# Gated linear attention in a one-core network kernel: chunk states replaced by scores of all tokens, small products moved between the weight products

## The chip, the core and the metric

The kernel runs on one core of a Trainium2 chip. TensorE (PE) multiplies, VectorE (DVE) and ScalarE (ACT) work element by element, SyncE (SP) issues the transfers; each works through its own queue in order and waits on semaphores of the others. The metric is the device time of one execution in microseconds (us), as the median of several.

## What is computed

A network of two transformer-like parts on 256 tokens of width 1024: two layers of feed-forward, attention or DeltaNet, and cross attention, then four layers, of which the third (i = 2) is the gated linear attention (GLA) that is changed. `first_block`, retention, convolution and MLP layers stand around it untouched.

```python
def gated_linear_scan(q, k, v, log_g, strict):      # heads 4, dk 128, dv 256, chunks of 64 of the 256 tokens
    c = jnp.cumsum(lg, axis=3)                       # inside a chunk
    c_last = c[:, :, :, -1:, :]
    q_dec, k_dec, k_end = q * jnp.exp(c), k * jnp.exp(-c), k * jnp.exp(c_last - c)
    scores = jnp.einsum("bhncd,bhnsd->bhncs", q_dec, k_dec)
    o_intra = jnp.einsum("bhncs,bhnsv->bhncv", jnp.where(mask, scores, 0.0), v)
    def step(state, inp):
        o = jnp.einsum("bhcd,bhdv->bhcv", qd, state)
        state = dec[..., None] * state + jnp.einsum("bhcd,bhcv->bhdv", ke, vv)
        return state, o
...
def gla(u, w_in, gate_w1, gate_w2, gate_b, norm_gain, w_out):
    q, k, v, r = jnp.split(u @ w_in, [kd, 2 * kd, 2 * kd + vd], axis=-1)
...
    def log_gate(d):
        logits = (u @ gate_w1[d]) @ gate_w2[d] + gate_b[d]
        return split_heads(jax.nn.log_sigmoid(logits.astype(F32)) / GLA_GATE_NORMALIZER, GLA_HEADS)

    o = bidirectional_scan(q, k, v, log_gate(0), log_gate(1))   # forward, and backward in flipped time
    o = merge_heads(rmsnorm_2(o, norm_gain)) * jax.nn.silu(r)
    return o @ w_out
```

## The kernel before

**Weight products.** Every large product runs over a stream of 836 weight tiles of 128 x 1024 float32 (512 KB). A tile is loaded into one of three buffers `SL`, ACT rounds it into `WH` (`hi`, L1866), DVE subtracts to get the rest `WL` (`lo`, L880), and PE multiplies high by high, high by low and low by high. A tile holds four blocks of 128 x 256 weights; a block is six matmuls of 256 columns (`multiply`), in the stages `g.v0` and `g.v1` two blocks together are six matmuls of 512 columns (`multiply_tok`). There are four `WH` and four `WL` buffers, so `hi(t)` waits until PE has done tile t - 4 (`s_block`), and in the queues of ACT and DVE the split of tile t + 3 stands where PE begins tile t (`walk`). A stage with kc = 8 goes through the blocks (j, k) of its output groups j; `outer` makes the first two or three groups go side by side.

**The GLA layer** is the stages `g.qk` (32 blocks: queries and keys), `g.v0`, `g.v1` (16 blocks each: values), `g.r` (32 blocks: gate r) and `g.o` (32 blocks: output), and small products in float32, each call of which is two records in the trace (a transpose one). In `tensor_program` `gla` first issues the gate's rank-16 product (`gt1`, 16 calls inside `g.qk`), then after `g.qk` the logits `gx`, then `g.v0`, `g.v1` and `g.r` with nothing between them (`through`), and then everything of the attention: 16 transposes, the scores `gp` inside a chunk, the products `gs` for the states, and for each of the four heads `go` (masked scores times values plus queries times six states, 64 columns each), and the sums of squares `gn`.

**The two other queues.** ACT and DVE make the decays in `slot`s, one at each odd k of `g.v0`, `g.v1` and `g.r`, in passes over 2048 columns (absolute value, exponential, logarithm L2498 to L2504; exponentials L2508 to L2513), DVE the running sums by eight scans (L1781), the products with queries and keys (L1771), masks and adds (L1800 to L1804), the states (L1821, L1824), the gate product (`gated`, L1228) and the head norms (L1834). `part_hi` (L2058) and `part_lo` (L1061) split the result of a head; `g.o` waits for `o_lo` of head k // 2 at its first group. `post_norm` then waits for the sum of squares of `g.o`, gathered by `add_squares` (L918, L921), `added` and `total`.

**Small banks.** `small` deals PSUM banks 4 to 6 in turn to the small products, and waits until the third last of them has been read.

Of the kernel before, what the change touches and what calls it, by code (L numbers as in the profile page):

```python
# [11 lines left out]
def layout_columns():  # L12
# [4 lines left out]
             ("wab", 128), ("gw1", 256), ("gb", 8), ("gn", 2), ("alog", 8), ("dtb", 8), ("rdl", 16),  # L17
# [32 lines left out]
def stage_table():  # L50
# [59 lines left out]
def build_program(nc, w, pk, cp, xT_in, mem_in, pos_in, out):  # L110
# [13 lines left out]
    with ctx:  # L124
# [84 lines left out]
        fin = Signal(sem("s_fin"), [("dn", 0), ("dn", 2)] + [("r0", j) for j in range(4)] + [("g", 0)]  # L209
# [20 lines left out]
        g_ln, g_cu, g_ee, g_eex = (Signal(sem(n), ["all"]) for n in ("s_g_ln", "s_g_cu", "s_g_ee", "s_g_eex"))  # L230
# [7 lines left out]
        hsq, hz = Signal(sem("s_hsq"), heads), Signal(sem("s_hz"), heads)  # L238
# [9 lines left out]
        g_kt = Signal(sem("s_g_kt"), [(d, x) for d in range(2) for x in ("ee", "en", "ec")])  # L248
        g_p = Signal(sem("s_g_p"), [0, 1])
# [8 lines left out]
        def tensor_program(p):  # L258
# [504 lines left out]
            def gla():  # L763
                VT, PTt, KT, T1, EC, EN, EE = PG[1], PG[8], PG[7], PG[2][0:16, 0:512], PG[4], PG[5], PG[9]
                SS = {}
                for d in range(2):
                    for n in range(3):
                        x = d * 3 + n
                        SS[d, n + 1] = BIG[:, 4096 + x * 1024:5120 + x * 1024] if x < 4 else PG[9][:, (x - 4) * 1024:(x - 3) * 1024]
# [8 lines left out]
                p.wait_ge(s_cp, 64)  # L778
                freed("gt1")
                for d in range(2):  # L780
                    for half in range(2):
                        bk = small(("gx", d, half))
                        for i in range(2):
                            at = d * 512 + (2 * half + i) * 128
# [47 lines left out]
                for hd in range(4):  # L832
# [13 lines left out]
                    if hd:  # L846
                        head_sums(hd - 1)
# [1936 lines left out]
```

## Time and profile before

| | us |
|---|---|
| median of 3 runs | 2923.65 (2921.19 to 2925.53) |
| the profiled execution | 2922.59 |
| its span, first to last instruction | 2920.8 |
| PE busy in it | 2741.9 |
| GLA layer, first matmul of `g.qk` to last of the closing sum (2124.28 to 2309.47) | 185.2 |

A busy PE is not a PE at its peak: matmuls overlap, so a matmul that is shown with 0.28 us is followed 0.12 us later by the next. What a product costs is read from start to start.

### The profile page before, as it was taken

To read this page: it belongs to the slowest core of one execution; us is meant where nothing else is said; L and a number is where in the kernel's file an instruction comes from. 1 tells how busy PE (TensorE), PEld (TensorE's weight loads), DVE (VectorE), ACT (ScalarE), POOL (GpSimd) and SP (SyncE) were. 2 spreads that over 40 slices of the span, in tenths; PEclk is the share of its full clock that TensorE was granted. 3 is DMA by queue.
4 is the path that set the end of the run, shared out by engine and by line. 5 is a ranking of instruction groups with operands and counts; after the bars stand their busy time and mean duration, and the time that the engine had idled before them with its cause. 6 is when DMAs were issued, how large, how long until landed. Compare 5 with 4: busy or idle time off the path is not lost. (4 is left out here: it accounts for less than half of the span.)

```text
span 2920.8 us, 49180 instructions
## 1 busy us (share of the span) xinstructions
PE 2741.9 (94%) x21134; PEld 2647.2 (91%) x21134; DVE 1841.7 (63%) x2375; ACT 1417.5 (49%) x1917; POOL 0.2 (0%) x4
## 2 busy tenths in 40 slices
PE   7999989999997898999998999989997899999998
PEld 7998889999996788999898999889977899989998
DVE  5657656656666646666645756967455586655764
ACT  5444535454465354545345465264453445445443
POOL 0000000000000000000000000000000000000000
PEclk9998999999998999999999999999997899999999
DMA  6553435555543133555544564136531355453463
GB/s 209 178 185 128 159 108 193 193 184 186 194 145 102 54 116 115 192 188 172 169 144 138 173 202 157 46 127 202 189 128 58 112 182 194 159 173 121 154 202 130
DMA packets 129001, 450.11 MB, mean 154 GB/s; under 512 B 20112, under 2 KB 20368, under 8 KB 128528
## 3 DMA queue, kind: packets, MB, share of 16 engines
q1 hardware_dynamic: 128784, 446.97, 46.6%
q8 instruction: 167, 2.74, 0.4%
q14 instruction: 50, 0.41, 0.0%
HBM read 445.47 MB, written 1.44 MB: 153 GB/s over the span
## 5 line engine op out<-in xcount | busy, mean ns | idle before, releaser
L260 PE MATMUL B<-R,WH 128*128 128x256 f32 x10432 | 2092.9, 284 | 70.4 <-DVE R L946 37.1
L260 PEld LDWEIGHTS B<-R,WH 128*128 128x128 f32 x10432 | 1692.8, 191 | 85.0 <-DVE R L946 27.5
L880 DVE TENSOR_TENSOR WL<-SL,WH 128x1024 fp32r<-128x1024 f32 x836 | 1011.3, 1223 | 770.6 <-ACT WH L1866 769.3
L260 PE MATMUL B<-R,WL 128*128 128x256 f32 x4480 | 1266.6, 283 | 0.0
L1866 ACT ACTIVATE WH<-SL 128x1024 fp32r<-128x1024 f32 x836 | 866.3, 1053 | 524.8 <-PE B L260 409.6
L260 PEld LDWEIGHTS B<-R,WL 128*128 128x128 f32 x4480 | 860.2, 192 | 0.0
L260 PE MATMUL B<-RB,WH 128*128 128x256 f32 x1984 | 556.6, 281 | 0.2 <-DVE WL L880 0.2
L260 PE MATMUL B<-RB,WL 128*128 128x256 f32 x1728 | 482.2, 279 | 0.0
L260 PEld LDWEIGHTS B<-RB,WH 128*128 128x128 f32 x1984 | 374.5, 189 | 0.7 <-DVE WL L880 0.4
L260 PEld LDWEIGHTS B<-RB,WL 128*128 128x128 f32 x1728 | 324.9, 188 | 0.0
L260 PE MATMUL B<-WH,R 128*128 128x512 f32 x480 | 160.3, 408 | 3.0 <-DVE WL L880 3.0
L260 PE MATMUL B<-PG 128*128 128x256 f32 (+5 forms) x704 | 143.8, 363 | 6.4 <-DVE PG L973 2.1
L260 PEld LDWEIGHTS B<-PG 128*128 128x128 f32 (+2 forms) x704 | 122.3, 212 | 20.9 <-issue 7.4
L1934 ACT ACTIVATE R<-X,PK 128x256 fp32r<-128x256 f32 x128 | 61.3, 505 | 117.9 <-DVE X L954 65.9
L2346 ACT ACTIVATE RB<-PG 128x512 fp32r<-128x512 f32 x64 | 40.5, 633 | 159.4 <-DVE PG L1470 159.4
L260 PEld LDWEIGHTS B<-WH,R 128*128 128x128 f32 x480 | 92.8, 193 | 27.4 <-DVE WL L880 5.1
L260 PE MATMUL B<-WL,R 128*128 128x512 f32 x240 | 97.0, 404 | 0.0
L260 PE MATMUL B<-PG,ONES 128*128 128x256 f32 (+1 forms) x242 | 73.2, 425 | 19.7 <-DVE PG L921 6.6
L2031 ACT ACTIVATE RB<-PG 128x512 fp32r<-128x512 f32 x44 | 27.9, 633 | 128.7 <-DVE PG L1038 128.7
L946 DVE SCALAR_TENSOR_TENSOR R<-X,PK,R 128x256 fp32r<-128x256 f32 x128 | 59.0, 482 | 29.1 <-ACT R L1934 29.1
L969 DVE TENSOR_TENSOR R<-PG,RB 128x512 fp32r<-128x512 f32 x108 | 73.9, 684 | 3.3 <-ACT RB L2031 2.8
L2028 ACT ACTIVATE PG<-PG 128x512 f32<-128x512 f32 x44 | 27.8, 632 | 90.3 <-DVE PG L1031 90.3
(289 smaller groups left out, 1586.5 us busy)
## 6 DMA issues: line engine op xcount, KB each, us to landing
SL<-in_w SPq DMA_DIRECT2D x836, 512.0 KB, 3.6
CP<-in_cp SPq DMA_DIRECT2D x5, 768.0 KB, 5.6
X<-in_xT SPq DMA_DIRECT2D x2, 512.0 KB, 6.6
PG<-in_mem SPq DMA_DIRECT2D x1, 1024.0 KB, 11.0
out<-X SPq DMA_DIRECT2D x1, 1024.0 KB, 3.9
PK<-in_pk SPq DMA_DIRECT2D x1, 598.5 KB, 3.9
dn_y<-PG SPq DMA_DIRECT2D x1, 256.0 KB, 2.2
PG<-dn_y SPq DMA_DIRECT2D x16, 16.0 KB, 1.8
```

Of the source, the lines that this page charges most:

```text
L260: return p.matmul(o, left, right, start=first, stop=final, skip_group_check=True)
L880: v.tensor_tensor(WL[t % NSPL][:, :], SL[t % NRAW][:, :], WH[t % NSPL][:, :].bitcast(F32), ALU.subtract).then_inc(s_lo, 1)
L946: v.scalar_tensor_tensor(R67[:, 2048 + c * 256:2304 + c * 256], X[:, cc(c)], gain(c), R67[:, cc(c)].bitcast(F32), ALU.mult, ALU.subtract). ...
L969: v.tensor_tensor(R03[:, hc(u)], d, RB[:, hc(u)].bitcast(F32), ALU.subtract).then_inc(hid_lo.sem, hid_lo.give((f, u)))
L1866: a.activation(WH[t % NSPL][:, :], SL[t % NRAW][:, :], ACT.Copy).then_inc(s_hi, 1)
L1934: a.activation(R67[:, cc(c)], X[:, cc(c)], ACT.Copy, scale=gain(c)).then_inc(h_hi.sem, h_hi.give((n, c)))
L2028: a.activation(s, s, ACT.Silu).then_inc(silu.sem, silu.give((f, u)))
L2031: a.activation(RB[:, hc(u)], PG[10][:, u % 4 * 512:u % 4 * 512 + 512], ACT.Copy).then_inc(hid_hi.sem, hid_hi.give((f, u)))
L2346: a.activation(RB[:, hc(x)], PG[10][:, x % 4 * 512:x % 4 * 512 + 512], ACT.Copy).then_inc(hid_hi.sem, hid_hi.give((f, x)))
```

## The change

The chunk states, the transposes and the scans go. The scores of every pair of the 256 tokens are made directly, and one product of 256 x 256 scores with the values gives a head.

- `gt1`: both directions in one product of 32 columns (8 calls for 16). `gx`: four calls, tokens on partitions and 512 features as columns; the bias is row 33 of the operand.
- Running sums over time (`running`) are 16 matmuls with masks of ones in `CP`; ACT reads them out of PSUM and makes `KE`, `EC` and the chunk ends `FT` (`decays`).
- `near`: scores inside 128 tokens, 8 calls a piece (the one with `EE` reaches over a chunk's edge). `far`: scores between the two halves of 128 tokens, 8 calls of 64 columns. `values`: four calls of 256 columns a head.
- All of them stand between blocks of `g.v0`, `g.v1` and `g.r`, and so do head sums, the inverse roots (two by two), normalization and gating; `g.o` has `outer` 2. On ACT and DVE passes are 512 and 1024 columns wide. The order of normalize and gate is turned.

```diff
-        outer = 2 if name == "c.o" else OUTER if name in ("f1.0.in", "r0.q", "c.in", "g.qk", "r3.q") or name.endswith(".up") else 0
+        outer = 2 if name in ("c.o", "g.o") else OUTER if name in ("f1.0.in", "r0.q", "c.in", "g.qk", "r3.q") or name.endswith(".up") else 0
...
+                def logits(x):
...
+                    mm(bk[:, :], T1[:, x % 2 * 128:x % 2 * 128 + 128], CP[0:33, hc(x // 2)]).then_inc(s_small, 1)
...
+                def running(d, hp):
...
+                    p.wait_ge(g_sp.sem, g_sp[d])
+                    for i in range(2):
+                        for tb in range(2):
+                            at = (2 * d + tb) * 512 + (2 * hp + i) * 128
+                            t = mm(bk[:, i * 256 + tb * 128:i * 256 + tb * 128 + 128], XL[:, at:at + 128],
+                                   CP[:, 1024 + d * 128:1152 + d * 128])
...
+                def near(d, hp):
...
+                    p.wait_ge(g_in.sem, g_in[d])
+                    for i in range(4):
+                        at = d * 1024 + (2 * hp + i // 2) * 256 + i % 2 * 128
+                        mm(bk[:, i * 128:(i + 1) * 128], KE[:, at:at + 128], EC[:, at:at + 128])
+                        e = EE[:, at // 2:at // 2 + 64]
+                        if d == 0:
+                            t = mm(bk[0:64, i * 128 + 64:i * 128 + 128], e, EC[:, at + 64:at + 128])
+                        else:
+                            t = mm(bk[64:128, i * 128:i * 128 + 64], e, EC[:, at:at + 64])
...
+                def far(hp):
...
+                            mm(bk[:, o + d * 64:o + d * 64 + 64], s, EC[:, at:at + 64])
+                            t = mm(bk[:, o + 64 - d * 64:o + 128 - d * 64], s, XC[:, d * 256 + hd * 64:d * 256 + hd * 64 + 64])
...
+                def values(hd):
+                    bk = small(("go", hd))
+                    p.wait_ge(g_p.sem, g_p[hd // 2])
+                    freed(("gd", hd // 2))
...
+                    for i in range(2):
+                        for s in range(2):
+                            f0 = s * 1024 + hd * 256 + i * 128
+                            t = mm(bk[:, cc(i)], VT[:, f0:f0 + 128], PT[:, hd * 512 + s * 256:hd * 512 + s * 256 + 256], s == 0, s == 1)
...
-                        for d in range(2):
-                            for c in range(8):
-                                t = mm(bk[0:16, cc(d)], pc("gw1", d * 128 + c * 16, 16), H[:, cc(c)], c == 0, c == 7)
+                        for c in range(8):
+                            t = mm(bk[0:32, 0:256], pc("gw1", c * 32, 32), H[:, cc(c)], c == 0, c == 7)
...
-                through(normed("g.v0"))
-                through(normed("g.v1"))
-                through(normed("g.r"))
-                for d in range(2):
-                    for tb in range(2):
...
-                            t = p.transpose(bk[:, hd * 128:(hd + 1) * 128], EE[:, at:at + 128], IDN)
...
-                            t = mm(bk[:, i * 128:(i + 1) * 128], EN[:, at:at + 128], EC[:, at:at + 128])
...
-                                t = mm(bk[:, cc(i)], KT[pr, at:at + 128], VT[pr, tb * 1024 + hd * 256:tb * 1024 + (hd + 1) * 256])
...
-                        for tb in range(2):
-                            mm(bk[:, i * 256 + tb * 128:i * 256 + (tb + 1) * 128], VT[:, tb * 1024 + f0:tb * 1024 + f0 + 128],
-                               PTt[:, hd * 256 + tb * 128:hd * 256 + (tb + 1) * 128], i == 0 and tb == 0, False)
-                        for d in range(2):
-                            for n in range(1, 4):
-                                ch = n if d == 0 else 3 - n
-                                q0 = d * 1024 + hd * 256 + ch * 64
-                                t = mm(bk[:, i * 256 + ch * 64:i * 256 + (ch + 1) * 64],
-                                       SS[d, n][:, f0:f0 + 128], EC[:, q0:q0 + 64], False, d == 1 and n == 3)
-                    t.then_inc(s_small, 1)
-                    if hd:
-                        head_sums(hd - 1)
...
+                for j, k in normed("g.v0"):
+                    if 1 <= k < 5:
+                        logits(k - 1)
+                    if k >= 6:
+                        running(0, k - 6)
+                for j, k in normed("g.v1"):
+                    if k in (1, 2):
+                        running(1, k - 1)
+                    if k in (6, 7):
+                        near(0, k - 6)
+                for j, k in normed("g.r"):
+                    x = 8 * j + k
+                    if x in (3, 5):
+                        near(1, x // 2 - 1)
+                    if x in (7, 9):
+                        far(x // 2 - 3)
+                    if x in (11, 12, 14, 15):
+                        values({11: 0, 12: 1, 14: 2, 15: 3}[x])
+                    if 17 <= x < 21:
+                        head_sums(x - 17)
...
+                def softplus(d):
+                    v.wait_ge(g_ln.sem, g_ln[d])
...
+                def decayed(d):
...
+                    v.tensor_tensor(KE[:, ds], KE[:, ds], K, ALU.mult).then_inc(V.sem, V.up())
+                    v.scalar_tensor_tensor(EC[:, ds], EC[:, ds], 128.0 ** -0.5, Q, ALU.mult, ALU.mult).then_inc(V.sem, V.up())
...
+                def farther(d):
...
+                for j, k in walk("g.v0"):
+                    if k == 5:
+                        softplus(0)
+                    if k == 7:
+                        softplus(1)
+                for j, k in walk("g.v1"):
+                    if k == 3:
+                        decayed(0)
+                    if k == 5:
+                        farther(0)
+                    if k == 7:
+                        decayed(1)
+                for j, k in walk("g.r"):
+                    x = 8 * j + k
+                    if x == 1:
+                        scores(0, 0)
+                        scores(0, 1)
+                    if x == 2:
+                        farther(1)
+                    if x in (5, 7):
+                        scores(1, x // 2 - 2)
+                    if x == 25:
+                        normalize(0)
+                        gate(0)
+                        normalize(1)
+                    if x == 26:
+                        rest(0)
+                        gate(1)
+                    if x == 27:
+                        normalize(2)
+                        rest(1)
+                    if x == 29:
+                        gate(2)
+                        normalize(3)
+                    if x == 30:
+                        rest(2)
+                    if k == 7:
+                        scaled_to("g.r", j, RG)
+                gate(3)
+                rest(3)
...
+                def decays(d, hp):
...
+                    a.activation(KE[:, at:at + 512], bk[:, :], ACT.Exp, scale=1.0 / 16)
...
+                for j, k in walk("g.v0"):
+                    if 1 <= k < 5:
+                        logits(k - 1)
+                    if k in (2, 4):
+                        exps(k // 2 - 1)
+                    if k in (3, 5):
+                        ln(k // 2 - 1)
+                    if k == 7:
+                        decays(0, 0)
+                tok_to("g.v0", 0, lambda tb: VT[:, tb * 1024:tb * 1024 + 512], True)
+                for j, k in walk("g.v1"):
+                    if k == 0:
+                        decays(0, 1)
+                    if k in (2, 3):
+                        decays(1, k - 2)
+                tok_to("g.v1", 0, lambda tb: VT[:, tb * 1024 + 512:tb * 1024 + 1024], True)
+                for j, k in walk("g.r"):
+                    x = 8 * j + k
+                    if x in (8, 10):
+                        far(x // 2 - 4)
+                    if x in (12, 13, 15, 16):
+                        values({12: 0, 13: 1, 15: 2, 16: 3}[x])
+                    if 18 <= x < 22:
+                        sd_of(("gn", x - 18), PG[2][:, cc(x - 18)], 256, 1.0 / 256)
+                    if x in (20, 22):
+                        freed(("gn", x - 20))
+                        freed(("gn", x - 19))
+                        inverse_root(PG[2][:, (x - 20) * 256:(x - 18) * 256], ("g", x - 20))
+                    if x == 23:
+                        silu(0)
+                        silu(1)
+                    if x == 25:
+                        silu(2)
+                    if x == 26:
+                        high(0)
+                    if x == 27:
+                        high(1)
+                    if x == 30:
+                        high(2)
+                silu(3)
+                high(3)
```

**PE at the end of `g.r`.** B is a PSUM bank, R67 the normed input, WH and WL the split weights, R45 the split result of the heads, PG scratch. Before:

```order
L260 MATMUL B1<-R67,WL3 128x256
L797 MATMUL B4<-PK,PG9 128x128 x4
L797 MATMUL B5<-PK,PG9 128x128 x4
L797 MATMUL B6<-PK,PG9 128x128 x4
L797 MATMUL B4<-PK,PG9 128x128 x4
L260 MATMUL B5<-PG4,PG5 128x128 x4
L260 MATMUL B6<-PG4,PG5 128x128 x4
```

And now, from the second group of `g.r`, where `values` of two heads stand:

```order
L260 MATMUL B5<-PG8,PG1 128x256 x4
L260 MATMUL B3<-R67,WH2 128x256 x2
L260 MATMUL B3<-R67,WL2 128x256
L260 MATMUL B3<-R67,WH2 128x256 x2
L260 MATMUL B3<-R67,WL2 128x256
L260 MATMUL B6<-PG8,PG1 128x256 x4
L260 MATMUL B3<-R67,WH3 128x256 x2
L260 MATMUL B3<-R67,WL3 128x256
```

What stood behind the last block of `g.r` now stands between its blocks; behind the last one comes `g.o`.

**ACT at the end of `g.r`.** SL is a loaded tile. Before:

```order
L1961 ACTIVATE BIG<-BIG 128x512 [waits s_bank0]
L1866 ACTIVATE WH1<-SL1 128x1024 [waits s_block,s_w1]
L1866 ACTIVATE WH2<-SL2 128x1024 [waits s_block,s_w2]
L1961 ACTIVATE BIG<-BIG 128x512 [waits s_bank1]
L2523 ACTIVATE PG7<-B4 128x512 [waits s_small]
```

And now, from the second inverse root on (L1884 is `hi`, L2535 `silu`, L2076 `part_hi`):

```order
L2171 ACTIVATE PG2<-PG2 128x512 [waits s_scalar]
L2535 ACT_TABLE_LOAD
L2535 ACTIVATE BIG<-BIG 128x512 [waits s_bank2]
L2535 ACTIVATE BIG<-BIG 128x512 [waits s_bank3]
L1884 ACTIVATE WH1<-SL1 128x1024 [waits s_block,s_w1]
L2535 ACTIVATE BIG<-BIG 128x512 [waits s_bank0]
L2076 ACTIVATE R45<-BIG 128x512 [waits s_gy] x2
L1884 ACTIVATE WH2<-SL2 128x1024 [waits s_block,s_w2]
L2076 ACTIVATE R45<-BIG 128x512 [waits s_gy]
L2535 ACTIVATE BIG<-BIG 128x512 [waits s_bank1]
L2076 ACTIVATE R45<-BIG 128x512 [waits s_gy]
L1920 ACT_TABLE_LOAD
```

All four splits of the heads, two passes of `silu` and two table loads stand between the splits of weight tiles.

## Rows read from the trace of the kernel before

**Rows 1.** The page: the span, and busy us, share and instructions of each engine.

```profile
span 2920.8 us, 49180 instructions
...
PE 2741.9 (94%) x21134; PEld 2647.2 (91%) x21134; DVE 1841.7 (63%) x2375; ACT 1417.5 (49%) x1917; POOL 0.2 (0%) x4
```

**Rows 2.** Stretches: us; busy PE, PEld, DVE, ACT, POOL; granted clock; DMA share, GB/s.

```profile
2124.28:2157.70 33.42, 33.42 (x230) 29.11 (x231) 22.05 (x36) 17.31 (x29) 0.00 (x0) 0.91 0.40 127
2157.70:2161.93 4.23, 4.23 (x18) 3.09 (x17) 0.69 (x1) 2.51 (x6) 0.00 (x0) 0.86 0.00 0
2161.93:2186.95 25.02, 25.02 (x97) 20.05 (x97) 15.14 (x14) 15.71 (x15) 0.00 (x0) 0.89 0.43 144
2186.95:2225.50 38.55, 27.11 (x205) 26.46 (x203) 25.81 (x27) 20.45 (x20) 0.00 (x0) 0.87 0.35 111
2225.50:2281.84 56.34, 46.08 (x228) 42.45 (x228) 17.81 (x39) 12.91 (x21) 0.00 (x0) 0.68 0.03 10
2281.84:2309.50 27.66, 26.82 (x198) 25.94 (x198) 15.65 (x20) 14.22 (x20) 0.00 (x0) 0.91 0.49 152
```

**Rows 3.** PE in order of time: start, us, engine, line, operation, count, [idle <-releaser].

```profile
2187.30 0.40 PE L260 MATMUL B<-R,WH 128*128 128x256 f32 x2
...
2197.46 0.40 PE L260 MATMUL B<-R,WH 128*128 128x256 f32 x2
...
2282.65 0.63 PE L260 MATMUL B<-R,WH 128*128 128x256 f32 x2
...
2283.29 0.63 PE L260 MATMUL B<-R,WH 128*128 128x256 f32 x2
```

**Rows 4.** PE in order of time: waits in the convolution's `c.o` (1929.67) and in GLA.

```profile
1929.67 0.67 PE L260 MATMUL B<-PG,ONES 128*128 128x256 f32 x2 [2.22 <-DVE PG L921]
...
2212.81 0.79 PE L260 MATMUL B<-R,WH 128*128 128x256 f32 x2 [5.22 <-DVE WL L880]
...
2281.84 0.79 PE L260 MATMUL B<-R,WH 128*128 128x256 f32 x2 [5.22 <-DVE R L1061]
```

**Rows 5.** PE in order of time: small products among weight products, and in GLA.

```profile
848.80 1.05 PE L260 MATMUL B<-CP,PG 128*128 128x128 f32 x8
849.61 0.48 PE L260 MATMUL B<-R,WH 128*128 128x256 f32 x2
...
2270.43 1.11 PE L260 MATMUL B<-PG 128*128 128x64 f32 x8
2271.38 1.00 PE L260 MATMUL B<-PG,BIG 128*128 128x64 f32 x8
...
2272.66 1.08 PE L260 MATMUL B<-PG,ONES 128*128 128x256 f32 x4
```

**Rows 6.** Weight loads of `gt1` and `gx`: min/median/max ns, first and last start.

```profile
L260 PEld LDWEIGHTS B<-H,PK x32: 93/97/98, 2147.7 to 2154.2; 128*16 128x16 f32 x32
...
L260 PEld LDWEIGHTS B<-PG,CP x16: 182/185/332, 2157.7 to 2160.9; 16*128 16x128 f32 x16
```

**Rows 7.** Groups of instructions, 2270 to 2310: shapes, count | busy us, mean ns | idle, releasers.

```profile
L880 DVE TENSOR_TENSOR WL<-SL,WH 128x1024 fp32r<-128x1024 f32 x8 | 9.7, 1224 | 7.2 <-ACT WH L1866 7.1
L1866 ACT ACTIVATE WH<-SL 128x1024 fp32r<-128x1024 f32 x8 | 8.4, 1058 | 2.6 <-PE B L260 1.7 <-DMA SL<-in_w 0.9
...
L1834 DVE SCALAR_TENSOR_TENSOR BIG<-BIG,PK,PG 128x256 f32<-128x256 f32 x8 | 3.5, 479 | 3.4 <-ACT PG L2153 3.4
L1061 DVE TENSOR_TENSOR R<-BIG,R 128x512 fp32r<-128x512 f32 x4 | 2.8, 693 | 2.8 <-ACT R L2058 2.8
L2058 ACT ACTIVATE R<-BIG 128x512 fp32r<-128x512 f32 x4 | 2.5, 630 | 5.7 <-DVE BIG L1834 5.7
...
L1902 ACT ACT_TABLE_LOAD x1 | 1.3, 1283 | 0.0
```

**Rows 8.** Stretches as in rows 2: one with PE waiting, one with PE full.

```profile
1142.00:1146.00 4.00, 0.88 (x7) 0.79 (x7) 2.83 (x5) 1.24 (x3) 0.00 (x0) 1.00 0.00 0
2246.00:2269.90 23.90, 23.90 (x107) 23.18 (x106) 1.38 (x2) 3.88 (x8) 0.00 (x0) 0.50 0.00 1
```

More of the change, by code:

```diff
@@ L770, in gla, with head_sums @@
+                def head_sums(hd):
+                    bk = small(("gn", hd))
+                    p.wait_ge(hsq.sem, hsq["g", hd])
+                    for c in range(2):
+                        t = mm(bk[:, 0:256], ONES[:, :], PG[3][:, hd * 512 + c * 256:hd * 512 + (c + 1) * 256], c == 0, c == 1)
+                    t.then_inc(s_small, 1)
                 for j, k in normed("g.qk", 17):
@@ L779, in gla @@
-                freed("gt1")
-                for d in range(2):
[L781 to L784, printed above, removed]
-                            t = mm(bk[:, cc(i)], CP[0:16, at:at + 128], T1[:, cc(d)])
-                        t.then_inc(s_small, 1)
-                through(normed("g.v0"))
-                through(normed("g.v1"))
-                through(normed("g.r"))
@@ new lines, in normalize, with gate @@
+                def normalize(hd):
+                    if hd % 2 == 0:
+                        v.wait_ge(fin.sem, fin["g", hd])
+                    freed(("go", hd))
+                    for c in range(2):
+                        s = O[:, hd * 512 + c * 256:hd * 512 + (c + 1) * 256]
+                        v.scalar_tensor_tensor(s, s, pc("gn", c), PG[2][:, cc(hd)], ALU.mult, ALU.mult).then_inc(V.sem, V.up())
+                def gate(hd):
+                    v.wait_ge(V.sem, V.n)
+                    v.wait_ge(g_silu.sem, g_silu[hd])
+                    v.tensor_tensor(O[:, hc(hd)], O[:, hc(hd)], RG[:, hc(hd)], ALU.mult).then_inc(gy.sem, gy.give(("g", hd)))
@@ new lines, in rest @@
+                def rest(hd):
+                    part_lo("g", hd, O[:, hc(hd)]).then_inc(o_lo.sem, o_lo.give(("g", hd)))
+                for j, k in walk("g.v0"):
[10 more added lines that the diff above has]
+                        decayed(1)
@@ L2520, in gla, with logits @@
-                for d in range(2):
-                    for tb in range(2):
-                        bk, free = had(("gkt", d, tb))
-                        a.activation(KT[:, hc(2 * d + tb)], bk[:, :], ACT.Copy).then_inc(free, 1)
-                for hd in range(4):
+                def logits(x):
+                    bk, free = had(("gx", x))
+                    a.activation(XL[:, hc(x)], bk[:, :], ACT.Relu, scale=-1.0)
+                    a.activation(AB_[:, hc(x)], bk[:, :], ACT.Abs).then_inc(free, 1)
@@ L2525, in gla, with far, values @@
+                def far(hp):
+                    bk, free = had(("gd", hp))
+                    a.activation(r3(PT[:, hp * 1024:(hp + 1) * 1024], 512)[:, :, 128:384], r3(bk[:, :]), ACT.Copy).then_inc(free, 1)
+                def values(hd):
                     bk, free = had(("go", hd))
-                    if hd:
-                        sd_of(("gn", hd - 1), PG[2][:, cc(hd - 1)], 256, 1.0 / 256)
+                    a.activation(PG[3][:, hc(hd)], bk[:, :], ACT.Square).then_inc(hsq.sem, hsq.give(("g", hd)))
@@ L2537, in gla, with silu, high @@
-                for j in range(4):
-                    a.wait_ge(gy.sem, gy["g", j])
-                    part_hi("g", j, O[:, hc(j)])
+                def silu(j):
+                    evacuated("g.r", j)
+                    a.activation(RG[:, hc(j)], RG[:, hc(j)], ACT.Silu).then_inc(g_silu.sem, g_silu.give(j))
+                def high(hd):
+                    a.wait_ge(gy.sem, gy["g", hd])
+                    part_hi("g", hd, O[:, hc(hd)])
+                for j, k in walk("g.v0"):
[7 more added lines that the diff above has]
+                        decays(0, 0)
```

302 lines of the change are left out of this document (94 added, 208 removed).

## The prediction

> **What bounds the kernel now.** I read the page first [rows 1]: PE is busy 2741.9 of 2920.8 us. A wait of ACT or DVE is worth nothing in itself; only PE's waits and PE's own work are. The GLA layer is 185.2 us (2124.28 to 2309.47), and its stretches [rows 2] show where it differs from the rest. What it must do at least is read from two points of the weight products [rows 3]: from 2187.30 to 2197.46 there are 29 triples of matmuls, 0.35 us each, so a block of six is 0.70 us and the layer's 128 blocks are 89.6 us. The other 95.6 us are the small products and waits. Half of that is one stretch, 2225.50 to 2281.84: 56.3 us in which no weight product runs and ACT and DVE are busy 13 and 18 us. There PE's clock is 0.68 on average, and 0.50 for 23.9 us together although PE is full [rows 8]; those are the 64-column products of `go`. A call of 64 columns costs as much as one of 128: eight records took 0.95 us at full clock (2270.43 to 2271.38), eight of 128 columns 0.81 us (848.80 to 849.61) [rows 5]. The last wait in this stretch is PE for `part_lo`, 5.22 us, behind inverse root, norm and splits; one of the same length stands in `g.r`, for the split of a weight tile that stood behind three 2048-column passes on ACT [rows 4].
>
> **The sum.** The layer is rebuilt from its first matmul to its last, in the order that the new queues show.
>
> *`g.qk`* takes 33.4 us [rows 2]. Of it `gt1` is 32 records over 2147.7 to 2154.2, 31 steps of 0.21, so 0.21 a record and 0.42 to 0.44 a call of 256 columns [rows 6]. It has 8 calls for 16: 3.5 us off. 29.9 stay. Its vector and scalar parts are covered by the rest of `g.qk`.
>
> *Weight products* of `g.v0`, `g.v1`, `g.r`, `g.o`: 96 blocks at 0.70 are 67.2 us.
>
> *Small products.* A call of 256 columns is 0.44, one of 128 is 0.20, one of 64 is 0.24 (above). `gx`: 4 calls of 512 columns, 3.5. `running`: 16 calls of 128, 3.2; the row at 848.80 is just this kind of product between blocks. `near`: 16 calls of 128 columns, 3.2, and 16 with 64 columns and 64 rows of output, which the trace does not have; taken as 0.20, 3.2, with bounds 0.10 and 0.24. `far`: 16 calls of 64, 3.8. `values`: 16 of 256, 7.0. Head sums: 8 of 256, 3.5. Together 27.4 us. Returning from each of 22 groups to the weight products costs about 0.08: the first pair after a small group shows 0.48 us for 0.40 [rows 3, 5]; 1.8 us. The closing sums stay as they are, about 2.1. The sum so far is 67.2 + 27.4 + 1.8 + 2.1 = 98.5 us, with PE never waiting.
>
> The 64-column stationary operand of `near` is where a page of the Trainium skill says more than the rows. Here a load of 16 columns takes 97 ns, and one of 16 rows with 128 columns 185 ns [rows 6]. TensorE: Matmul & The Clock Gate, section LDWEIGHTS, says that a load costs by its columns and not by its rows; by that rule the trace agrees in direction, since only fewer columns made it shorter, though 16 columns did not cost an eighth. By the rule the 16 calls would be 1.6 us instead of 3.2, and the total 1.6 lower.
>
> *PE's new waits.* I followed the three queues, with hi 1.06, lo 1.22, 512-column passes 0.63 to 0.69, a normalization of two 256-column passes 0.9, a table load 1.28 [rows 7]. (a) In `g.v0` PE asks for `running(0, 0)` 12 us after the stage's start, and ACT has then done three pairs of 512-column passes, exponential, logarithm and two tile splits; DVE's sum ends 0.7 late. (b) Before `g.o`: from the last head sum PE has 11 to 12 blocks left, 8.4 us. Meanwhile ACT takes standard deviations and two inverse roots (3.4), loads a table (1.3), makes two silu (1.2) and a hi (1.0), then DVE lo (1.2), normalize, gate, normalize, rest (0.9 + 0.7 + 0.9 + 0.7): 11.3 us. PE waits 3.0 where it waited 5.2. (c) The fourth tile of `g.o` has its hi behind silu(3), part_hi(3) and a second table load, themselves behind gate and split of each head: about 11.8 us after (b), when PE has 8.4 of work: 3.4. (d) With `outer` 2 the squares of `g.o` are added one tile later, behind a lo. The convolution's `c.o` has exactly this order and shows 2.22 [rows 4]. The waits are 0.7 + 3.0 + 3.4 + 2.2 = 9.3 us. The rest of ACT's and DVE's new work is hidden by PE's 0.7 us blocks; the nearest is `far`, for which DVE is ready some 2 us before PE.
>
> *The clock.* The weight products take 0.64 for 0.35 a triple at half clock [rows 3]. In the old layer the half clock followed PE waits of 5 us and the 64-column series. Now those series are 1.9 us long between blocks, and two waits of 3 us are left; one between 1142 and 1146, 3.1 us long, left the clock at 1.00, others like it did not [rows 8]. I take one short fall, 1.6 us; bounds 0 and two of 6.8 us, 6.2 us.
>
> Together 29.9 + 98.5 + 9.3 + 1.6 = 139.3 us, against 185.2: 45.9 us less. The profiled execution's own time would be 2922.59 - 45.9 = 2876.7; the median of the runs is 1.1 above it, so the forecast is **2878 us**. Nothing outside the layer changes, except which phase of the clock the later layers meet (1 or 2 us either way).
>
> **Rivals.**
>
> *Almost no waits* (a chance of 0.07). If table load and silu are quicker to come or DVE gets ahead, (a) to (c) vanish and the clock stays up: 8.7 us less, 2869; with `near` at 0.10 a call, 2868. Against it: the chains (b) and (c) are made of passes whose lengths the trace has, and their order is fixed.
>
> *The half clock over part of the interleaved stretch* (0.10). The clock could fall in `near`, `far` or the logits on 33 rows as it fell in the old series. For it: 23.9 us at 0.50 with PE full, and `gx` on 16 rows, after which it fell too (0.86 and 0.89 in rows 2). Against it: between them now stand weight products that are full. Ten to thirty us at half cost 5 to 14 us more: 2883 to 2895 with what else spreads.
>
> *Slower than before: the half clock over all of it* (0.03). This is the one mechanism that could eat the gain. If the clock is 0.50 from `logits` to the last head sum, 64 blocks cost 0.58 more each, 37 us, and the 27.4 us of small products double: 64.5 in all, less 1.6 already counted, 2941 us. It outweighs the gain from 71% of that stretch on (45.9 of 64.5). The row that speaks for it is the 23.9 us [rows 8]; that the clock was 1.00 around 848.80, where products of 128 columns stand among blocks, speaks against it.
>
> *Splits come late in more places* (0.08). ACT has some 26 us of work in the 37 us of `g.v0` and `g.v1`, and in the old `g.r` three wide passes in a row cost PE 5.22 at one tile [rows 4]. Two or three such waits more: 2888 to 2894. Against it: the widest pass is now 1.06 us.
>
> *It doesn't do what it says*: the queues show PE's products between the blocks and nothing of them behind `g.r`; I leave no chance for it.
>
> **How the numbers follow.** The forecast has 0.72, with its own range of 2869 to 2887: down by 9 for the waits and `near`, up by 5 for the clock and 4 for waits mis-sized. The range of 2868 to 2889 adds the low rival and the lower part of the two middle ones, and leaves out under 0.2. A measurement can tell about 0.2%, 6 us, from no change. All but the third rival are faster by more: faster 0.96, slower 0.03, and 0.01 for a case between.
>
> **What would show it.** The stretch between `g.r` and `g.o` shrinks from 56.3 us to one PE wait of about 3 us, for DVE's part_lo line. Six to eight small groups of PE stand inside `g.r`, and from first matmul to closing sum the layer is 139 us. A wait of PE for the WL line stands three tiles into `g.o`, about 3.4, and one of 2.2 before the added squares. The granted clock is 1.00 through most of the layer. The forecast is wrong if PE waits in `g.v0` or `g.v1` for more than 1 or 2 us, if the triples there take 0.64, or if `near` and `far` cost other than 1.6 and 1.9 us a group.

## The result, and the profile after

The changed kernel takes 2889.78 us in the median of four runs (2886.24 to 2892.77), the kernel before 2924.59 (2921.19 to 2927.38): a ratio of 0.9881, with a 95% interval of 0.9864 to 0.9898. That is 34.8 us less where 45.9 were forecast, and 0.8 us above the forecast's range. The profiled execution took 2890.59 us, of which 2888.8 are its span.

The page of the changed kernel, which answers to [rows 1]:

```profile
span 2888.8 us, 48977 instructions
...
PE 2724.2 (94%) x21046; PEld 2629.4 (91%) x21046; DVE 1822.6 (63%) x2346; ACT 1411.3 (49%) x1924; POOL 0.2 (0%) x4
```

The span fell by 32.0 us. Four stretches of the changed kernel, one behind the other, run from the first product of `g.v0` to the closing sum, the last of them from the first matmul of `g.o`; the fifth is the whole layer (columns as in [rows 2]):

```profile
2162.30:2176.00 13.70, 13.70 (x48) 7.72 (x47) 5.50 (x5) 10.96 (x15) 0.00 (x0) 1.00 0.26 87
2176.00:2204.00 28.00, 28.00 (x162) 23.01 (x161) 16.71 (x21) 13.12 (x23) 0.00 (x0) 1.00 0.33 112
2204.00:2243.63 39.63, 36.88 (x269) 34.67 (x268) 15.59 (x22) 18.73 (x29) 0.00 (x0) 1.00 0.27 91
2243.63:2276.25 32.62, 27.81 (x198) 26.62 (x198) 18.40 (x23) 16.96 (x23) 0.00 (x0) 0.90 0.45 146
2133.37:2276.25 142.88, 135.32 (x884) 118.87 (x884) 78.24 (x105) 77.21 (x118) 0.00 (x0) 0.96 0.35 118
```

The layer takes 142.9 us where it took 185.2: 42.3 us less, of 45.9 forecast. The 56.3 us without a weight product [rows 2] are gone, and the clock, 0.68 to 0.91 in the stretches of the old layer, is 0.96 on average. So the layer accounts for 3.6 us of what is missing. But it **starts** at 2133.37 where it started at 2124.28, and what follows it takes 612.6 us where it took 611.3. Some 10.3 us of the gain were lost in stretches to which the change does nothing.

PE in the layer, changed kernel, in order of time (columns as in [rows 3]): the waits and the new small groups.

```profile
2163.77 1.12 PE L260 MATMUL B<-CP,PG 33*128 33x512 f32 x2
2164.82 0.50 PE L260 MATMUL B<-WH,R 128*128 128x512 f32 x1
...
2175.72 1.13 PE L260 MATMUL B<-CP,PG 128*128 128x128 f32 x8
...
2190.57 2.67 PE L260 MATMUL B<-PG 128*128 128x128 f32 x16
2193.17 0.50 PE L260 MATMUL B<-WH,R 128*128 128x512 f32 x1
...
2215.52 1.89 PE L260 MATMUL B<-PG 128*128 128x256 f32 x8
2217.06 0.59 PE L260 MATMUL B<-R,WH 128*128 128x256 f32 x2
...
2243.63 0.79 PE L260 MATMUL B<-R,WH 128*128 128x256 f32 x2 [2.75 <-DVE R L1071]
...
2255.55 0.48 PE L260 MATMUL B<-R,WH 128*128 128x256 f32 x2 [1.71 <-DVE WL L890]
...
2271.13 1.19 PE L260 MATMUL B<-PG,ONES 128*128 128x256 f32 x2 [2.63 <-DVE PG L931]
...
2275.12 1.13 PE L260 MATMUL B<-PG,ONES 128*128 128x256 f32 x4 [0.47 <-ACT PG L2007]
```

A group ends where the next row starts. `logits` is 2163.77 to 2164.82, 1.05 us; a group of `near` 2190.57 to 2193.17, 2.60 us, the one size that is far off; `values` 1.54. In `g.v0`, `g.v1` and `g.r` PE waits for nothing. In place of the two waits of 5.22 us [rows 4] there are two in `g.o`, 2.75 and 1.71.

**Where the other 10 us go.** No wait of PE accounts for them: on the page PE's busy time fell by 17.7 us, where the layer's alone fell from 162.7 (the sum of [rows 2]) to 135.3, by 27.4. Weight products cost more. A stretch ahead of the layer in both kernels, in which PE is full, does weight products only and has the clock at 1.00, shows it in the count behind PE (kernel before, then changed):

```profile
660.00:760.00 100.00, 100.00 (x860) 100.00 (x859) 67.33 (x72) 45.77 (x54) 0.00 (x0) 1.00 0.58 187
```

```profile
660.00:760.00 100.00, 100.00 (x852) 100.00 (x851) 66.06 (x72) 46.59 (x54) 0.00 (x0) 1.00 0.57 185
```

860 products fall into the 100 us before, 852 after (two or three of them are under way when it begins). In order of time one sees the pace itself. Kernel before:

```profile
699.89 0.40 PE L260 MATMUL B<-R,WH 128*128 128x256 f32 x2
...
702.34 0.40 PE L260 MATMUL B<-R,WH 128*128 128x256 f32 x2
```

Changed kernel:

```profile
700.00 0.40 PE L260 MATMUL B<-R,WH 128*128 128x256 f32 x2
...
706.01 0.40 PE L260 MATMUL B<-R,WH 128*128 128x256 f32 x2
```

Seven triples in 2.45 us are 0.350 each, 0.1167 us a product, as in [rows 3]; seventeen in 6.01 are 0.3535, 0.1178 us a product. The duration of one row (0.28 us from start to modelled end) hides this; only starts show it. Ahead of the layer both traces have the same 15,591 matmuls in the same order, 13,825 of them weight products of 256 columns, so each step from one start to the next can be set against its counterpart. The weight products at full clock and without a wait take 12.3 us more in the changed kernel; steps with a wait of PE take 2.7 us less, and those at half clock 0.7 less. That makes the 9.1 us. It is less than 13,825 times 0.0011 us, 15 us, since the kernel before runs at 0.1178 us too in some stretches, from 80 to 220 us among others.

### The profile page after: what moved, and what is told of

Read it like the earlier page. It is cut to its first block and busy times, and to the rows that moved or that the text cites. A ratio compares the mean times of both kernels' runs of the same rounds, so it can differ in the third digit from the quotient of the medians.

```text
span 2888.8 us, 48977 instructions
## 1 busy us (share of the span) xinstructions
PE 2724.2 (94%) x21046; PEld 2629.4 (91%) x21046; DVE 1822.6 (63%) x2346; ACT 1411.3 (49%) x1924; POOL 0.2 (0%) x4
## 5 line engine op out<-in xcount | busy, mean ns | idle before, releaser
L890 DVE TENSOR_TENSOR WL<-SL,WH 128x1024 fp32r<-128x1024 f32 x836 | 1011.0, 1223 | 785.9 <-ACT WH L1884 784.9
L1884 ACT ACTIVATE WH<-SL 128x1024 fp32r<-128x1024 f32 x836 | 866.1, 1052 | 553.9 <-PE B L260 444.8
L260 PE MATMUL B<-PG 128*128 128x256 f32 (+6 forms) x672 | 132.3, 344 | 4.5 <-DVE PG L983 2.1
L260 PEld LDWEIGHTS B<-PG 128*128 128x128 f32 (+2 forms) x672 | 109.4, 192 | 19.8 <-issue 5.7
```

Source lines behind the costliest of these rows:

```text
L260: return p.matmul(o, left, right, start=first, stop=final, skip_group_check=True)
L890: v.tensor_tensor(WL[t % NSPL][:, :], SL[t % NRAW][:, :], WH[t % NSPL][:, :].bitcast(F32), ALU.subtract).then_inc(s_lo, 1)
L1884: a.activation(WH[t % NSPL][:, :], SL[t % NRAW][:, :], ACT.Copy).then_inc(s_hi, 1)
```

## The experiments

The change has one more edit, to the table of constants PK:

```
-             ("wab", 128), ("gw1", 256), ("gb", 8), ("gn", 2), ("alog", 8), ("dtb", 8), ("rdl", 16),
+             ("wab", 128), ("gw1", 256), ("gn", 2), ("alog", 8), ("dtb", 8), ("rdl", 16),
```

The first theory (A): this takes eight columns (`gb`) out of PK. PK is allocated ahead of the weight tiles and behind those of R, so SL, WH and WL start 32 bytes earlier, while the tiles of R stay; where they lie against each other sets the pace. (No trace shows an address; the places here follow from the order and the sizes in the kernel.) The rival (B): the two executions or programs differ in something else. For the layer itself, the questions were what makes `near` dear, and whether the waits come from the places of the steps in the queues.

### The place of the weight tiles

e1 is the changed kernel, e2 the kernel before, each with this edit:

```
-             ("eps", 1), ("invf", 1), ("ident", 128)]
+             ("eps", 1), ("invf", 1), ("ident", 128), ("pad", 8)]
```

> The changed kernel with eight unused columns put back behind the last constant of PK, so that SL, WH and WL start 32 bytes further, where they started in the kernel before; no instruction is added, taken or moved. Theory A (where WH and WL begin against R sets the pace of back-to-back weight products: 0.1167 us each before, 0.1179 us each after, in stretches in which neither kernel waits): the pace goes back to 0.1167, and the time falls from 2889.8 by about 2100/0.1179 x 0.0012 = some 10 to 14 us, to 2876 to 2880. Rival B (the pace differs because the program or its execution differs in another way, such as where its code lies or how the two runs fell): the pace stays at 0.118 and the time within 3 us of 2889.8.

> The kernel before with eight unused columns added behind the last constant of PK: SL, WH and WL start 32 bytes further, on a multiple of 64 bytes, as they do in the changed kernel. Theory A: the pace of back-to-back weight products goes from 0.1167 to 0.1179 us and the time rises from 2924.6 by 10 to 14 us, to 2935 to 2939. Rival B: the pace stays at 0.1167 and the time within 3 us of 2924.6.

e1 took 2882.35 us (2875.5 to 2885.49), 0.9868 of the kernel before (0.9852 to 0.9885), and 7.4 less than the changed kernel, where 10 to 14 were expected. e2 took 2957.98, a ratio of 1.0131 (1.0112 to 1.0150): **eight columns that nobody reads cost the kernel before 35 us**, as much as the whole change to GLA brings. The same stretch in e1:

```profile
660.00:760.00 100.00, 100.00 (x860) 100.00 (x859) 67.69 (x72) 46.41 (x54) 0.00 (x0) 1.00 0.58 189
```

and in e2:

```profile
660.00:760.00 100.00, 100.00 (x836) 100.00 (x835) 65.50 (x71) 44.20 (x51) 0.00 (x0) 1.00 0.57 185
```

e1 has the old pace back. e2 has neither of the two: its products start every 0.1200 us. So A holds against B, but the expectation for e2, 10 to 14 us, was wrong by a factor of three: it took e2 to land where the changed kernel is, since both start on a multiple of 64 bytes.

e6 to e8 and e11 move only WH and WL, with SL and PK where the changed kernel has them:

```
-        WH = [sb(f"WH{i}", 1024, F32R) for i in range(NSPL)]
-        WL = [sb(f"WL{i}", 1024, F32R) for i in range(NSPL)]
+        WH = [sb(f"WH{i}", 1056, F32R)[:, 24:1048] for i in range(NSPL)]
+        WL = [sb(f"WL{i}", 1056, F32R)[:, 24:1048] for i in range(NSPL)]
```

> The changed kernel with only the start of the WH and WL tiles moved, by columns of wider tiles: they start 32 bytes past a multiple of 128 (in the changed kernel 64 bytes past one, in the kernel before 96, and in e2 on one; paces 0.1178, 0.1167, 0.1200 us). The tiles of R start on a multiple of 128 in all. Theory A says the start alone sets the pace, so the pace is one value through most stretches and differs from 0.1178; if it is distance from R's residue that counts, 32 and 96 are alike: 0.1167. Rival B' (what counts is where SL or PK lie, that is, the splits and not the products): the pace stays at 0.1178, since those have not moved.

> As e6, but WH and WL start 80 bytes past a multiple of 128: is a step of 16 bytes seen? If only blocks of 32 bytes count, the pace is that of the changed kernel, 0.1178. If finer steps count, it lies elsewhere, between 0.1133 (the shortest that any stretch of these runs shows) and 0.1200.

> As e6, but 48 bytes past a multiple of 128. If only blocks of 32 bytes count, it is as e6 at 32 bytes. If finer steps count, it differs from e6.

> As e6, with WH and WL starting 112 bytes past a multiple of 128. e7 (80 bytes) had the pace of 64 bytes, 0.1178 us; if 16 bytes within a block of 32 don't matter, this one has that of 96 bytes, 0.1167 us, and since SL and PK have not moved, this also tells e1's pace from a shift of SL or PK.

e10 moves everything, R and the weights alike:

```
+        sb("P0", 8)
         X = sb("X", 2048)
```

> The changed kernel with 32 unused bytes in front of the first tile, so that every tile starts 32 bytes further: R at 32, WH and WL at 96 past a multiple of 128. If the distance between R and WH sets the pace (64 in the changed kernel), it stays 0.1178 us. If WH's own place sets it, it is 0.1167 us, as in e1, where WH and WL lie at the same addresses but R at 0.

Then three to settle what was left, all on one chip; e13 is e6 with `[:, 8:1032]`, e15 is e1 with 40 columns for 8:

> As e6, with WH and WL 96 bytes past a multiple of 128, while SL and PK lie as in the changed kernel. If the distance of WH and WL from R sets the pace, it is 0.1167 us in most stretches, and the time is that of e1, 2880 to 2884 us. If e1's pace came from SL, it stays 0.1178 us and the time that of the changed kernel, 2889.8.

> The changed kernel once more, unchanged, on the chip of e13. Expected 2887 to 2892 us and a pace of 0.1178 us; e13 less e14 is the price of the distance, 7 to 12 us. If the two agree within 2 us, e1's shorter time was chance.

> As e1, with 40 unused columns in place of 8: SL, WH and WL lie 128 bytes further than in e1. If the effect repeats every 128 bytes, the pace is 0.1167 us and the time 2876 to 2886 us; if its period is longer (256 bytes and more), the pace may be another, 0.1178 to 0.1206 us.

All of them together. "Moved" is the start of WH0 against that in the changed kernel, in bytes, with R in place; tile to tile is the step from WH0 to WH1; then PE's count from 660 to 760, and the median us. The kernels before and changed, e1, e2, e13 and e14 were run four times or more, e15 twice, the others once. e5 to e8 ran on a chip on which the kernel before took 2932.0 us in its one run; their times are to be held against that one, and the argument goes by the counts.

| kernel | moved | tile to tile | products | us |
|---|---|---|---|---|
| before | +32 | 4096 | 860 | 2922.0 to 2924.6; 2932.0 beside e5 to e8 |
| e2 (code of before) | +64 | 4096 | 836 | 2958.0 |
| changed | 0 | 4096 | 852 | 2889.8 |
| e14, changed again | 0 | 4096 | 852 | 2892.5 |
| e1 | +32 | 4096 | 860 | 2882.4 |
| e15 | +160 | 4096 | 854 | 2901.3 |
| e10 | 0 (all tiles, R too, +32) | 4096 | 851 | 2892.8 |
| e7 | +16 | 4224 | 852 | 2898.5 |
| e13 | +32 | 4224 | 856 | 2882.7 |
| e11 | +48 | 4224 | 841 | 2915.4 |
| e6 | +96 | 4224 | 841 | 2916.6 |
| e8 | +112 | 4224 | 831 | 2926.5 |

What follows:

- e13 against e14, on the same chip: 2882.68 (2880.64 to 2887.49) against 2892.47 us (2890.69 to 2894.87), the two ranges apart. **The place of WH and WL alone is worth 9.8 us**; SL and PK have not moved. The size is that of the missing part, and it is lost at the same place: the layer's first product stands 9.6 us earlier in e13 than in e14:

```profile
2124.80 0.80 PE L260 MATMUL B<-R,WH 128*128 128x256 f32 x2 [3.05 <-DVE R L956]
```

```profile
2134.39 0.51 PE L260 MATMUL B<-R,WH 128*128 128x256 f32 x2 [3.05 <-DVE R L956]
```

- Not all of it is the pace itself. Step by step over the whole kernel, as above, these two traces differ by 12.8 us: 7.3 in weight products at full clock, 3.5 in steps at half clock, 2.7 in waits, the rest against them. For the changed kernel and e1 it is 11.7, 5.7 and -1.7 of 15.0. Whether the shift brings the other parts, or they vary from one execution to the next, one trace of each does not tell.
- It is a place **against tiles ahead of them**. In e10 WH and WL have the very addresses of e1, and R has moved along: the pace is that of the changed kernel. That R is the tile that counts is argued, since R is what these products read besides; e10 moved every other tile with it. The stretch in e10:

```profile
660.00:760.00 100.00, 100.00 (x851) 100.00 (x851) 66.33 (x71) 45.95 (x53) 0.00 (x0) 1.00 0.58 186
```

- 128 bytes is not a period: e15 is e1 and 128 bytes more, and where e1 has 0.1167 us but for a few stretches at 0.1178, e15 lies between 0.1173 and 0.1200 from stretch to stretch. e13 and e1, both moved by 32 bytes but with another step between the tiles, have 0.1171 and 0.1167.
- My expectation for e6, that 32 and 96 bytes past a multiple of 128 are alike, fell: 841 products, 0.1192 us. So did those that 16 bytes don't matter (e8 as e6, e11 as e13): 831 for 841 products, and 841 for 856. From the changed kernel to e7, 16 bytes made no difference. The slowest, e8:

```profile
660.00:760.00 100.00, 100.00 (x831) 100.00 (x830) 64.97 (x70) 44.86 (x52) 0.00 (x0) 1.00 0.57 186
```

- Within one kernel the pace can change between two values: e1 runs at 0.1178 from 1964 to 2023 us and in some other stretches, and elsewhere at 0.1167, and the changed kernel twice at 0.1133, from 2313 to 2369 and from 2723 to 2750 us. No run here controls that. Six triples of the first take 2.04 us:

```profile
2313.79 0.39 PE L260 MATMUL B<-R,WH 128*128 128x256 f32 x2
...
2315.83 0.39 PE L260 MATMUL B<-R,WH 128*128 128x256 f32 x2
```

The Trainium skill (TensorE: Matmul & The Clock Gate, section Step-by-step: what each phase is for) says that the two operands come over read ports of their own, and that a load of weights takes nothing from the running product. That rule gives no reason for the place of the tiles to change a pace; e13 and e14 show that it does. Whether reads of the two operands meet in the memory, or an engine's writes meet them, no run here tells.

### The small products of `near`

e3 takes the four 128-column products of a group first, and e4 leaves the four narrow ones out, so that its output is another:

```
                         mm(bk[:, i * 128:(i + 1) * 128], KE[:, at:at + 128], EC[:, at:at + 128])
+                    for i in range(4):
+                        at = d * 1024 + (2 * hp + i // 2) * 256 + i % 2 * 128
                         e = EE[:, at // 2:at // 2 + 64]
```

> The changed kernel, in near() the four products of 128 columns of a group first and then the four of 64 columns, in place of taking turns; a group took 2.60 us where 1.6 was forecast. If changing between the two widths is what costs, the group falls to 1.6 to 1.9 us. If the small product costs by itself, whatever stands beside it (its weight load, its column offset, two records each), the group stays at 2.5 to 2.7 us.

> The changed kernel without the 64-column products of near() (16 of its 32 calls): the part of the scores between the two halves of a block is left as the larger product gives it, so the output is another. Measures what the 128-column products cost alone. If these cost 0.10 us a record as the ones of running() do (8 records in 0.81 us), a group falls from 2.60 to 0.8 us, and the layer by 4 x 1.8 = 7.2 us; then the small ones cost 0.22 us a record. If the large ones here are dearer (PG4 and PG5 are read as both operands), a group stays over 1.2 us.

PE in e3, then in e4: a group and the row behind it.

```profile
2190.04 1.66 PE L260 MATMUL B<-PG 128*128 128x128 f32 x16
2191.64 0.50 PE L260 MATMUL B<-WH,R 128*128 128x512 f32 x1
```

```profile
2189.83 1.05 PE L260 MATMUL B<-PG 128*128 128x128 f32 x8
2190.64 0.48 PE L260 MATMUL B<-WH,R 128*128 128x512 f32 x1
```

A group is 2.60 us with the two widths taking turns, 1.60 sorted, and 0.81 without the narrow ones. So the narrow products add 0.79 us when sorted, 0.20 for each of the four calls, which is what the forecast took, and **taking turns** adds another 1.0 us a group. The group in e3 by shapes (2190.04 to 2191.64, columns as in [rows 7], weight columns behind the star) shows that the 0.20 is no price of the narrow call itself:

```profile
L260 PE MATMUL B<-PG 128*128 128x128 f32 x8 | 1.1, 275 | 0.0
L260 PE MATMUL B<-PG 128*64 128x64 f32 x8 | 0.7, 228 | 0.0
```

Without the length of the last record, seven steps are left of each: 0.78 us of the wide, 0.46 of the narrow. From start to start a wide record takes 0.11 us and a narrow one 0.058, so a narrow call is 0.12; the rest is the step from the last wide record to the first narrow one, 0.205, the second narrow one, 0.106, and the step back to the weight products, 0.152. In the changed kernel these dear steps come with every pair: 0.205 and 0.107, then 0.151 and 0.213, together 0.68 us for a wide and a narrow call, where two steps of 0.11 and two of 0.058 would be 0.34. There a narrow product also writes into columns that the wide one just before it has written, and in e3 three calls stand between; the step into the narrow ones is 0.205 us in both, so that is not what costs. And it is the weight columns that halve the step: `far`, with 128 of them and 64 moving columns, keeps 0.11 a record.

In e3 the layer is 139.1 us (2132.97 to 2272.05), 3.8 less; e3 and e4 took 2885.63 and 2883.40 us in one run each. The rule that a load costs by its columns (the Trainium skill, TensorE: Matmul & The Clock Gate, section LDWEIGHTS (loading the stationary operand)), weighed in the prediction, would have made a narrow call half as dear as a wide one; the steps in e3, 0.058 and 0.11 us, agree with it. What it does not give is the price of a change of width, and without that the group could not be forecast.

### The waits around `g.o`

e5 moves `normalize`, `gate`, `high` and `rest` one to two blocks of `g.r` earlier on DVE and ACT. On DVE:

```
-                    if x == 25:
-                        normalize(0)
...
+                    if x == 23:
+                        normalize(0)
+                        gate(0)
+                        normalize(1)
```

> The changed kernel with the steps between the head sums and g.o placed one to two blocks of g.r earlier on VectorE and ScalarE (normalize, gate, the two halves of R45). VectorE stands idle from 2235.95 to 2239.44 while TensorE later waits 2.75 us for L1071 and 1.71 us for L890. If the places in the program make those waits, both go: g.o follows g.r without a wait, and the layer (142.9 us) falls by up to 4.5 us. If the chain root, table load, silu, first half, rest is too long whatever its place, the first wait stays over 2 us.

The waits did not go. In e5:

```profile
2239.69 0.50 PE L260 MATMUL B<-R,WH 128*128 128x256 f32 x2 [1.06 <-DVE R L1071]
...
2251.61 0.47 PE L260 MATMUL B<-R,WH 128*128 128x256 f32 x2 [3.18 <-DVE WL L890]
```

The first wait fell by 1.7 us and the second rose by 1.5: freed time, given back twelve us later. The layer is 141.6 us (2131.66 to 2273.28), 1.3 less than in the changed kernel. ACT in e5, in order of time, shows why:

```profile
2245.74 0.63 ACT L2535 ACTIVATE BIG<-BIG 128x512 f32<-128x512 f32 x1 [2.50 <-DVE BIG L983]
2247.20 0.64 ACT L2076 ACTIVATE R<-BIG 128x512 fp32r<-128x512 f32 x1 [0.83 <-DVE BIG L1811]
2247.86 1.28 ACT L1920 ACT_TABLE_LOAD   x1
2249.15 2.95 ACT L1884 ACTIVATE WH<-SL 128x1024 fp32r<-128x1024 f32 x3
```

Three splits stand in ACT's queue behind the last group's silu, which waits 2.50 us for DVE's reading of the last bank of `g.r`, behind its half of R45, and behind a table load. The last head's features are needed only twelve blocks into `g.o`. e9 is e5 and puts them behind the first split of `g.o`, on ACT and likewise on DVE:

```
-                silu(3)
-                high(3)
-                logs()
-                for j, k in to_post("g.o", 18):
-                    pass
+                for x, _ in enumerate(to_post("g.o", 18)):
+                    if x == 0:
+                        silu(3)
+                        logs()
+                    if x == 2:
+                        high(3)
```

> e5, and in g.o the last head's steps moved behind its first tile: ScalarE's Silu of the fourth group, its half of R45 and the table load come after the first split of g.o in place of before it, VectorE's with them. In e5 the first wait fell from 2.75 to 1.06 us, and the one for L890 rose from 1.71 to 3.18 us. If it is the splits of the next tiles that stand in ScalarE's queue behind the Silu of the fourth group (it stands 2.50 us for L983 there, then loads a table), the wait of 3.18 us goes, and g.r to g.o has under 1.5 us of waits in all. If the tiles' landings or free buffers hold them, the wait stays at 2 to 3 us.

The waits in e9:

```profile
2240.14 0.51 PE L260 MATMUL B<-R,WH 128*128 128x256 f32 x2 [1.06 <-DVE R L1071]
...
2249.54 0.51 PE L260 MATMUL B<-R,WH 128*128 128x256 f32 x2 [0.65 <-DVE R L1071]
...
2264.74 0.67 PE L260 MATMUL B<-PG,ONES 128*128 128x256 f32 x2 [2.21 <-DVE PG L931]
```

The wait for L890 is gone; one of 0.65 us for the last head's own half is what is late next. 1.71 us stay of what were 4.46. The layer is 138.1 us (2131.59 to 2269.69), 4.8 less than in the changed kernel. e5 and e9 were run once each (2888.49 and 2885.21 us), so their verdict rests on these rows and not on the times.

### All three together

> The three things together: e9's order behind the head sums, e3's order in near(), and WH, WL and SL 32 bytes further as in e1. If each acts alone: from 2882.4 (e1) less 4.0 (near) less about 3.5 (the waits of 2.75 and 1.71 us but for one rest) = some 2875 us. If the freed time is given back at the next wait, 2879 to 2882.

2872.44 us (2870.32 to 2878.35), 0.9839 of the kernel before (0.9811 to 0.9866), and some 17 us below the changed kernel, the runs of the two well apart. The layer takes 132.4 us (2125.14 to 2257.55). That is 2.6 us less than the 2875 expected if each part acts alone, so pace, `near` and waits add, and nothing is given back that the spread of the runs would show.

## Why the prediction was wrong, point by point

**The step that failed** is its last one: "Nothing outside the layer changes, except which phase of the clock the later layers meet (1 or 2 us either way)". The sum was made for the layer, and the remaining 2735.6 us of the span were carried over as they were. They became 2745.9. The first edit of the diff, eight columns of PK gone, moved every weight tile against R; that was costed at nothing, without a word. What the runs showed in its place: the weight products ahead of the layer take 12.3 us more for the shift, 9.1 with waits and clock. With the weight tiles 32 bytes further, as before, the changed kernel takes 2882.4 (e1) or 2882.7 us (e13): inside the range of 2868 to 2889, and 4 to 5 above the forecast.

**Within the layer** the order of work, the waits and the clock came as forecast, one price was missing, and the total was 142.9 us for 139.3:

- `near` was the mis-sized term: 2.60 us a group for 1.6, 4.0 us in all. The price of changing width from call to call was not in the sum, and the bounds of 0.10 and 0.24 a call did not hold the 0.45 that a narrow call came to. By itself it is 0.12, near the lower bound; that sorted groups come to the forecast 1.60 is luck, a narrow call taken too dear and two changes of width taken at nothing. `running`, taken from a row of this very kind, came out at 0.81 as forecast.
- The other groups nearly cancel. `logits` 1.05 us for 0.88, 0.7 more over four; `values` 1.54 for 1.75, 0.8 less; `far` 1.70 for 1.9, 0.4 less; the head sums 0.67 for 0.88 a head, 0.8 less. Going back to the weight products costs about 0.08 us behind `running` and `far`, 0.11 behind `logits` and `near`, but 0.19 behind `values` and head sums: 2.9 us for 1.8.
- The waits: (a) 0 for 0.7, (b) 2.75 for 3.0, (c) 1.71 for 3.4, (d) 2.63 for 2.2, so 7.1 for 9.3. Each stands at the place and for the line that was named. That (b) and (c) hang together through ACT's queue, the prediction used; e5 shows it from the other side.
- `g.qk` took 28.9 us for 29.9.
- One reading was wrong: the wait between 1142 and 1146 was taken not to lower the clock [rows 8], but the stretch ends too soon to tell. The clock fell 4.4 us later, in a second wait as long. The kernel before:

```profile
1150.00:1158.00 8.00, 6.43 (x22) 5.08 (x23) 3.46 (x7) 2.16 (x7) 0.00 (x0) 0.57 0.00 0
```

- The clock: 1.00 through the interleaved stretch and 0.90 over the 32.6 us of `g.o`, about 6.5 us at half, so up to 3.3 lost where 1.6 was taken.
- The pace, 0.1178 for 0.1167 us, is 0.7 us on the 96 blocks. Together 4.0 + 0.7 - 0.8 - 0.4 - 0.8 + 1.1 - 2.2 - 1.0 + 1.7 + 0.7 = 3.0 us of the 3.6. The remaining 0.6 I can't assign.

**The rivals.** None came true. The half clock over part of the stretch, or all of it, is refuted by the 1.00 of the rows above. Splits late in more places: the changed kernel has one wait for L890 in the layer, as forecast. The time fell in that rival's region (2888 to 2894) by another cause, which the times alone could not have told; the row counts do.

## What to carry to other kernels

Before a gain that went missing is looked for in the code that changed, compare a stretch that did not: the count of products in 100 us in which PE is full is the quickest look. A table of constants that grows or shrinks shifts every tile behind it, so a change of layout is an edit with a price of its own, and the same kernel with a few unused columns belongs beside it as a control. And when waits are moved by reordering, the next one in line on the feeding engine decides what is kept: here the first reordering brought little (e5) until the last head's steps left the way of the splits.

## What the runs showed of the hardware that I had not expected

- The pace of back-to-back products of 256 columns, at full clock and with no wait, lay between 0.1167 us (e1) and 0.1207 (e8) in one and the same stretch, by nothing but where the tiles of WH and WL start and how far apart they lie, and a step of 16 bytes can be enough (e6 against e8, e11 against e13). It cost the kernel before 35 us to move SL, WH and WL by 32 bytes (e2).
- The pace can hold one of two values for tens to hundreds of microseconds and then change (e1: 0.1167 and 0.1178; the changed kernel: 0.1178 and twice 0.1133). The shortest, 0.1133, would be worth some 60 to 80 us over the 18,600 products if it could be held, an estimate from these two paces; no layout tried here held it.
- Products of 128 and of 64 weight columns that take turns cost 0.68 us for a wide and a narrow call, where their own steps make 0.34: 1.0 us more for a group of eight calls than sorted by width (e3).
- In a row of its kind a float32 product of 64 weight columns and 64 moving columns takes 0.058 us a record, two records a call, and one of 128 weight columns 0.11, whether its moving columns are 128 or 64 (e3, `far`).
